# Decode-step kernel: queries' units before keys' units, decode ticks from the third key unit on

## The reference, cut to what matters

```python
h = rms_norm(x, kv_norm); proj = h @ kv_w
k = rms_norm(proj[keys], k_norm); v = proj[values]; logf = log_sigmoid(proj[forget] + f_bias)
qz = rms_norm(x, norm_g) @ w_q
q = rms_norm(qz[queries], q_norm); z = qz[gate]
s = q k^T / 8 + (c_q - c_k)          # c: cumulative sum of logf; masked: key position <= query's
o = softmax(s) @ v
out = (o * silu(z)) @ w_out
```

## Time and profile before

| | |
|---|---|
| median of three runs | 2490.41 us |
| profiled execution, its own time | 2492.78 us |
| its span | 2490.9 us |
| PE, DVE, ACT, POOL busy, share of the span | 89%, 53%, 38%, 43% |
| granted TensorE clock, mean | 0.958 |
| HBM read, written | 386.8 MB, 43.9 MB |

### The profile page before, as it was taken

How to read it: one execution, slowest core, us unless ns; L and a number is a source line. 1 busy time by engine, 2 the same in 40 slices (tenths; PEclk the granted TensorE clock), 3 DMA queues, 4 the chain that set the end, 5 groups by cost and what they waited for, 6 DMA issues and landing times.

```text
span 2490.9 us, 47081 instructions
## 1 busy us (share of the span) xinstructions
PE 2227.7 (89%) x16540; PEld 1915.5 (77%) x16540; DVE 1316.3 (53%) x1892; ACT 949.9 (38%) x1617; POOL 1076.7 (43%) x715
## 2 busy tenths in 40 slices
PE   5999999999339998979999999978888888898999
PEld 3999999999139998969999777745555455557998
DVE  4689888988690016566785111124443534444332
ACT  4556655665461013222222121424444344453121
POOL 0698899889673114443233333222222211211231
PEclk7999999999789999989999999989999998999999
DMA  3222222221143121133323778999999988972112
GB/s 112 65 69 78 78 65 68 80 76 63 37 126 119 44 102 43 66 119 111 117 76 121 267 266 332 331 369 397 348 378 391 358 334 328 399 288 106 50 60 83
DMA packets 137487, 430.96 MB, mean 173 GB/s; under 512 B 23889, under 2 KB 40658, under 8 KB 136162
## 3 DMA queue, kind: packets, MB, share of 16 engines
q1 hardware_dynamic: 121554, 375.94, 41.3%
q0 software_dynamic: 13168, 41.58, 4.7%
q10 hardware_dynamic: 2592, 11.14, 1.1%
HBM read 386.81 MB, written 43.87 MB: 173 GB/s over the span
## 4 chain that ended last, share of the span: by engine, by line
PE 58%; POOL 15%; DVE 11%; issue 8%; ACT 6%; DMA 2%; ACTq 0%; SPq 0%; POOLq 0%; DVEq 0%
POOL ACC L1346 7%; PE PS L602 6%; PE PS L600 6%; PE PS L601 6%; PE PS L698 5%; PE PS L700 5%; PE PS L699 5%; PE PS L821 4%; PE PS L765 4%; PE PS L874 3%; PE PS L901 3%; PE PS L889 2%; POOL ML L1376 2%; PE PS L608 2%; POOL WL L1319 2%
## 5 line engine op out<-in xcount | busy, mean ns | idle before, releaser
L1319 POOL TENSOR_TENSOR WL<-RAW,WH 128x1024 fp32r<-128x1024 f32 (+1 forms) x121 | 306.0, 2529 | 601.1 <-ACT WH L954 596.4
L1656 DVE SCALAR_TENSOR_TENSOR PS<-UX,CWT,PS 128x1024 f32<-128x1024 f32 (+1 forms) x672 | 466.2, 781 | 0.0
L633 PE MATMUL PS<-HH,WH 128*128 128x384 f32 (+1 forms) x1152 | 378.6, 329 | 20.7 <-DVE HL L1642 20.7
L635 PE MATMUL PS<-HH,WL 128*128 128x384 f32 (+1 forms) x1152 | 377.4, 328 | 0.0
L634 PE MATMUL PS<-HL,WH 128*128 128x384 f32 (+1 forms) x1152 | 377.3, 328 | 0.0
L1346 POOL TENSOR_TENSOR ACC<-ACC,PROD 128x1088 f32<-128x1088 f32 x112 | 284.7, 2542 | 31.3 <-ACT PROD L1006 25.1
L698 PE MATMUL PS<-GH,WH 128*128 128x384 f32 (+1 forms) x792 | 271.6, 343 | 26.4 <-DVE KC L1768 12.1
L700 PE MATMUL PS<-GH,WL 128*128 128x384 f32 (+1 forms) x792 | 263.1, 332 | 0.0
L699 PE MATMUL PS<-GL,WH 128*128 128x384 f32 (+1 forms) x792 | 262.1, 331 | 0.0
L633 PEld LDWEIGHTS PS<-HH,WH 128*128 128x128 f32 x1152 | 217.3, 189 | 24.7 <-issue 13.7
L954 ACT ACTIVATE WH<-RAW 128x1024 fp32r<-128x1024 f32 (+1 forms) x121 | 131.4, 1086 | 252.5 <-PE PS L602 217.0
(11 more groups left out here) (213 smaller groups left out, 4309.3 us busy)
## 6 DMA issues: line engine op xcount, KB each, us to landing
KV<-ck SPq DMA_DIRECT2D x256, 512.0 KB, 6.7
KV<-cv SPq DMA_DIRECT2D x256, 512.0 KB, 6.7
RAW<-wA SPq DMA_DIRECT2D x48, 512.0 KB, 3.3
RAW<-wP SPq DMA_DIRECT2D x16, 640.0 KB, 4.0
zT_scr<-ZS ACTq DMA_DIRECT2D x16, 544.0 KB, 2.7
Z<-zT_scr SPq DMA_DIRECT2D x16, 544.0 KB, 3.6
RAW<-wB SPq DMA_DIRECT2D x17, 512.0 KB, 3.2
RAW<-wO SPq DMA_DIRECT2D x16, 512.0 KB, 3.2
```

The lines of the kernel that those rows point to most:

```text
L633: pe.matmul(out, WH[w][:, kk], HH[:, k, a:b], start=k == 0, stop=False)
L635: mm = pe.matmul(out, WL[w][:, kk], HH[:, k, a:b], start=False, stop=k == KD - 1)
L1319: pool.tensor_tensor(WL[s][:, 0:n], RAW[s][:, 0:n], WH[s][:, 0:n].bitcast(F32), ALU.subtract).then_inc(s_lo, 1)
L1656: i = dve.scalar_tensor_tensor(out=o, in0=x, scalar=w[:, j:j + 1], in1=o, op0=ALU.mult, op1=ALU.add)
```

## The change

- The constants U_Q and U_K change places: the eight query units run before the eight key units. Weights' places, gains, scales and what is kept of the sample rows follow.
- 120 ticks instead of 72 lie in the units, listed by unit in UNIT_TICKS: 15 in the key units (2 to 3 in each from the third on), 41 in the value units, 64 in the gate units. 168 instead of 216 follow from the prompt stage's first slot on.
- The first batch has its new rows' scores at tick 15 instead of 1 (the new keys are complete only then), and its product with the new rows' values in a step of its own, `first_new`, at tick 68, with small tiles of its own (PTN0, OE0, OT0, RID0), since the values are complete only then. Its result is copied by `decode_heads(0)` at tick 71.
- The norm of queries and keys works in place in PSUM banks 0 to 2 (NCHAIN) instead of in SBUF (RS3); ACT takes one square root over 1088 columns instead of three; PE's next `norm` waits for DVE's product instead of ACT's root. FL now lies in the last part of SC.
- ACT's queue stores the normed rows, in `sample_columns`, not SP's. POOL loads the raw weights of the key units too. SP issues the first four page loads after the last query unit's weights.
- In ACT and DVE the ticks of a key unit stand before that unit's norm or scaling.
- On POOL the pads, the forget biases of batches 1 to 3 and `load_keys(0)` move, the last behind a wait for the first batch's end (`s_os`).

```diff
-U_CONV, U_OUT, U_PLE, U_F, U_K, U_Q, U_V, U_Z, U_W, U_TAIL = 0, 48, 64, 72, 73, 81, 89, 97, 105, 113
+U_CONV, U_OUT, U_PLE, U_F, U_Q, U_K, U_V, U_Z, U_W, U_TAIL = 0, 48, 64, 72, 73, 81, 89, 97, 105, 113
...
+        NCHAIN = PS[:, 0:3, :].rearrange("p a n -> p (a n)")[:, 0:R]
...
-        def unit_ticks(u):
-
-            if u < U_V + 2:
-                return 0, 0
-            return (4 * (u - U_V - 2), 4) if u < U_Z else (24 + 6 * (u - U_Z), 6)
-
-        SPOTS = {0: (), 4: (1, 3, 5, 7), 6: (1, 2, 3, 5, 6, 7)}
+        UNIT_TICKS = (0, 0, 2, 2, 2, 3, 3, 3) + (0, 1, 6, 6, 7, 7, 7, 7) + (8,) * PAIRS
+        SPOTS = {0: (), 1: (7,), 2: (3, 7), 3: (2, 5, 7), 4: (1, 3, 5, 7), 5: (1, 3, 4, 6, 7), 6: (1, 2, 3, 5, 6, 7),
+                 7: (1, 2, 3, 4, 5, 6, 7), 8: (0, 1, 2, 3, 4, 5, 6, 7)}
...
+        NEW_AT = (15,) + (1,) * (DB - 1)
+        I_FIRST = T_B + 32
+
+        T_UNITS, T_LEAD, T_END = sum(UNIT_TICKS), 4, T_B * DB + 4
+        H_UNITS = sum(i % T_B < 16 or 18 <= i % T_B < 34 for i in range(T_UNITS)) // 4 * 4
...
-            def store_normed(p):
-
-                sp.wait_ge(s_kn, p + 1)
-                sp.dma_start(kT[p] if p < PAIRS else qT[p - PAIRS], KN[:]).then_inc(s_kst, 16)
...
             def norm(p):
 
                 pe.wait_ge(s_sq3, p + 1)
-                atleast(pe, s_rs, p)
-                colsum(pe, 0, SQ3, w=BONES).then_inc(s_n, 1)
+                atleast(pe, s_kn, p)
+                for a, b in ((0, 512), (512, 1024), (1024, R)):
+                    mm = pe.matmul(NCHAIN[:, a:b], BONES, SQ3[:, a:b], start=True, stop=True)
+                mm.then_inc(s_n, 1)
...
+            def first_new():
+
+                pe.wait_ge(s_vr, PAIRS)
+                pe.wait_ge(s_dv, 18)
+                for y in range(4):
+                    mm = pe.matmul(PS[32 * y:32 * y + 32, 6, 0:4 * HD], PTN0[:, 32 * y:32 * y + 32],
+                                   VNW[:, 4 * HD * y:4 * HD * y + 4 * HD], start=True, stop=True)
+                mm.then_inc(s_fn, 1)
...
             def sample_columns(p):
 
                 act.wait_ge(s_kn, p + 1)
-                if p == PAIRS:
+                act.dma_start(qT[p] if p < PAIRS else kT[p - PAIRS], KN[:]).then_inc(s_kst, 16)
+                if p == 0:
                     act.wait_ge(s_pad2, 1)
...
             for p in range(2 * PAIRS):
-                weights_hi(U_K + p + 1)
+                weights_hi(U_Q + p + 1)
+                ticks(U_Q + p)
                 if p >= 2:
                     sample_columns(p - 2)
...
-                if U_V <= u + 3 < U_W:
+                if U_K <= u + 3 < U_W:
                     pool.wait_ge(s_lo, u + 2)
                     pool.dma_start(RAW[(u + 3) % 2][:, 0:KD * P], wB[wb(u + 3)]).then_inc(s_rawp[(u + 3) % 2], 16)
...
             pool.wait_ge(s_lo, U_W)
             pool.wait_ge(s_vst, 32 * PAIRS)
+            pool.wait_ge(s_os, 1)
             load_keys(0)
...
-                dve.reciprocal(RS3[:], RS3[:]).then_inc(s_rc, 1)
+                dve.reciprocal(NCHAIN, NCHAIN).then_inc(s_rc, 1)
...
             for p in range(2 * PAIRS):
+                ticks(U_Q + p)
                 atleast(dve, s_kn, p - 1)
-                scaled(KC[p % 2], U_K + p, 1, s_kc)
+                scaled(KC[p % 2], U_Q + p, 1, s_kc)
```

More of the change, by code:

```diff
@@ L531, in forget_back @@
                 sp.dma_start(FL[0:H, :], lfT).then_inc(s_fin, 16)
-            for u in range(U_F, U_V):
+            for u in range(U_F, U_K):
                 raw(u, wB[wb(u)], u % 2)
@@ L537, in _ @@
                     sp.dma_start(xS, X2[:]).then_inc(s_xs, 16)
-                if u == U_K + 4:
+                if u == U_Q + 4:
                     forget_store()
-                if u == U_K + 5:
+                if u == U_Q + 5:
                     forget_compact()
[L542 to L557, removed]
+            sp.wait_ge(s_xs, 16)
+            sp.wait_ge(s_gl, KD)
+            pages(0)
+            pages(1)
+            forget_logs()
+            forget_back()
+            pages(2)
+            pages(3)
             def raw_out(m):
@@ L1094, in unit @@
                     if not (end and l == 1):
-                        hi_next(u0, s, i, KD * P if end else SLOT, gained=end, less=PAIRS * l)
+                        hi_next(u0, s, i, KD * P if end else SLOT, gained=end, less=3 * PAIRS // 2 * l)
                     act.wait_ge(s_gate, KD * l + m + 1)
@@ L1222, in forget_exp, with ticks @@
                 act.activation(FC_E[:], FC_E[:], ACT.Exp).then_inc(s_fe, 1)
+            def ticks(u):
+                for k in range(KD):
+                    i = tick_after(u, k)
+                    if i is not None:
+                        decode_tick(i)
             for p in range(2 * PAIRS):
-                weights_hi(U_K + p + 1)
+                weights_hi(U_Q + p + 1)
+                ticks(U_Q + p)
                 if p >= 2:
@@ L1242, in _ @@
                     norm(2 * PAIRS - 1)
-                for k in range(KD):
-                    i = tick_after(u, k)
-                    if i is not None:
-                        decode_tick(i)
+                ticks(u)
             silu(PAIRS - 1)
@@ L1518, in _ @@
                     forget_out()
+                    scores_pad()
                 if p == PAIRS + 6:
```

142 lines of the change are left out of this document (88 added, 54 removed).

## The result

The kernel after takes 2527.9 us in the median (2526.6 to 2531.0, four runs) against 2489.9 for the kernel before beside it: a ratio of 1.0146 [1.0132, 1.0160]. It is slower by 38 us by the medians, 36 by the ratio, where +15 was forecast. The side is right, the size is off by more than a factor of two. The execution profiled after has a span of 2525.3 us against 2490.9, so the trace has 34.4 us to explain.

What follows compares the result with a forecast made beforehand. PE was taken to bound the units, with DMA time to spare, while the softmax chain idles PE in the prompt stage. Units +70 us and prompt stage -55 gave +15, forecast 2505 us; 8 in 10 between 2479 and 2528.

Steps and rivals of the forecast that it cites:

- what bounds each stretch: Units bound by PE with spare DMA time; in the prompt stage PE idles 81 us for the softmax chain, not pages.
- the sign: Whole kernel: slower, by 15 us or 0.6%; chance of slower 0.60, same 0.14, faster 0.26.
- Rival A: Prompt stage: ticks there cost more than their PE work, so the kernel gets faster, -13 us, 2477 us; chance 0.26.
- PE work of a tick: Units: 48 added ticks at 1.2 us of PE work each, +57.6 us.
- Pages: Units: page loads of dense gate units exceed the DMA rate, with a ring of four buffers; +9 us, bounds 0 and +30.
- rival B: Units: pages bind there, +30 us instead of +9, so +36, 2526 us; chance 0.20 together with C.
- Single bank set: Query, key and value units share banks and wait for DVE's scaling; with row maximum and forget scan, +3 us together.
- Rival C: Prompt stage: softmax chain rules all items, a removed tick gives 0.4 us; +37, 2527 us; chance 0.20 together with B.
- the -55 us of the prompt stage: Prompt stage: 48 ticks removed; ordinary ticks -41, batch changes -5, entry -9 us.
- Entry: Prompt stage's first item falls from 19.0 to about 10 us, its first ticks needing no page: -9 us (0 to -10).
- Items with ordinary ticks: Prompt stage: a removed tick gives 0.85 us over all, none in items of 896 and 1024 keys: -41 us.
- batch changes: Prompt stage: five batches instead of six pass their row maximum there: -5 us (0 to -6).

Runs made afterwards that it cites:

- experiment 6: Kernel before with six sample batches instead of eight and SP's wait at half group 184 of 192, so 144 prompt-stage ticks instead of 216: 2429.5 us, ratio 0.9748.
- experiment 1: Kernel after, with SP's wait for the last head pair's scores after half group 248 instead of 240 of 256: 2519.5 us, ratio 1.0105.
- experiment 3: Kernel after with the kernel before's tick counts (72 in the units, none in key units), all else kept: 2493.3 us, ratio 1.0011.
- experiments 5 and 10: Kernel before with 48 ticks in the units, none in value units: 2478.9 us; then 52, seven in each of the last four gate units: 2474.9 us.
- 84 ticks: Kernel after with 84 ticks in the units (20 value, 64 gate, no key) and SP's wait at half group 248: 2522.2 us, ratio 1.0128.
- the shifted kernel before: Kernel before with every prompt-stage tick due 0.7 of a slot earlier, nothing else: 2504.3 us, ratio 1.0049.
- experiment 2: Kernel after with one tick moved from the fifth gate unit to the last value unit, putting the third batch's row maximum inside a unit: 2528.1 us, ratio 1.0151.

## Why the prediction was right or wrong

**Right: what bounds each stretch, and the sign.** The units grew by 66.3 us, 1.38 for each of the 48 ticks: their full PE work and the stalls at unit ends. A tick taken from the prompt stage gives back less, because it filled the chain's gaps: 0.87 in experiment 6, and in experiment 1, with SP's wait gone, 614.3 - 571.8 = 42.5 us or 0.89, the entry in it. By the ratios the loss of 36 us splits into 3 for the order alone (experiment 3), 23 for the 48 ticks at their new places (3 to 1), and 10 for SP's wait (1 to the kernel after). The prices alone give 48 x (1.38 - 0.87) = 24.5 us. The two agree, but the placing of ticks moves single runs by 12 us and more, so this is not a proof to the microsecond. The opposite direction (experiments 5 and 10) confirms the sign, not the 0.87. Rival A, faster, has fallen.

**"PE work of a tick", right within 10%**: 57.6 forecast, +61.8 measured in PE's busy time. Key units with two ticks last 17.45 us where 17.8 was forecast.

**"Pages", over-sized**: 9 forecast, 2.1 us of PE's waits measured in the units. The DMA engines are at 0.99 there with 375 GB/s, and the ring of four buffers suffices; rival B has fallen. That 375 GB/s over 95 us and, in the stage of 52 ticks, 379 over 616 us were moved speaks again against the limit of 358 that the prediction quoted from the Trainium skill (DMA: Bandwidth & Descriptors, "Where 436 GB/s comes from"), at least for one core that runs alone.

**"Single bank set", +3 forecast and 2.4 measured, by luck.** Two more stalls were to cost 3.3 us and one row maximum 1.5. PE's waits for the scaling fell by 2.8 instead (12.1 to 9.3), and its waits for the first exponential rose by 5.2 (0.8 to 6.0), since the new one fell on a unit's first spot, behind ACT's work for the unit just ended. That was priced as an average one. With PE's work and the pages' 2.1 this makes up the 66.3 us.

**Rival C, the chain takes over**, lies between: the idle time in the stage did rise by 15 us, but without SP's wait the stage gave back twice the 0.4 a tick. Its 2527 us, and the end of the stated range at 2528, were met by the sum of other causes.

**The step that failed: the -55 us of the prompt stage.** The stage and the gap ahead of it gave back 34.3 us in the trace (37.0 less 2.7), so this sum is 21 us too large and carries nearly the whole error of 23. Two things are wrong in it.

*No term for SP's queue.* The prediction followed the page loads past the moved work in the units, and read SP's waits for buffers in the stage, but not the one row below them, the 8.3 us for the prompt's scores. That wait is tied to the prompt's progress, the page loads behind it to the ticks' progress; whoever changes the rate between the two (216 / 128 = 1.69 ticks a slot to 168 / 128 = 1.31) has to check it. It grew to 32.2 us and costs 8.4 us (experiment 1).

*What a tick gives back, priced too high.* Without SP's wait the stage and the gap still gave back only 39.8 us. "Entry": -9 forecast. The first item fell by 12.3 us, but the pages that it no longer waited for were waited for one and two items later. PE's waits from 1696 to 1741 us:

```profile
PE PS L824 <- DMA KV<-cv: 5.7, 3, 3.6
PE PS L761 <- DMA KV<-ck: 2.6, 2, 1.6
PE PS L803 <- ACT SC L1228: 1.4, 1, 1.4
PE PS L764 <- DMA KV<-ck: 1.1, 1, 1.1
```

The first four items together went from 48.6 to 42.9 us, and 2.7 more were lost between the last unit and the stage: 3 us won, not 9. "Items with ordinary ticks" and "batch changes": -41 and -5 forecast, 0.85 a tick and the changes on top. Experiment 6 gives 0.87 *with* its two batch changes, so that the two terms together should have been about -42; which of them was too large these runs do not tell.

**Open.** Why 84 ticks lie some 23 us above a straight line from 72 (experiment 3) to 120 (experiment 1), and why the shifted kernel before is slower. What experiment 2's edit is worth, and what the last 2 us in the end stage are, stay open too.

## What to carry to other kernels

Work that fills the gaps of a latency chain is cheap where it is, and full price in a stretch whose engine is never idle. Before moving it, price one piece at both places (here 1.38 against 0.87 us), by a run that drops pieces in one of them. When two progressions share an in-order queue, every wait in it that belongs to one of them is a bound on the other, and a change of their relative rate moves it; list such waits even if they cost nothing now. And where filler is dealt out by a formula, count what falls on which item, and deal it first to the items whose chain has gaps: a tick cost 0.29 to 0.54 us in a long item here and 1.08 to 1.27 in a short one. A shift of 0.7 of a slot was worth 24 us at one count, against 38 for the whole change.

## What was unexpected of the hardware

A single wait of 5.3 us, in a stretch where PE is otherwise always busy, was followed by 3.3 us of gapless matmuls at a clock of 0.50 and 4 us at 0.68. Before it and after it the clock is 1.00. The first item of the stage stands at 0.50 in the kernel after (0.55 before), behind 12.5 us in which PE was busy for two thirds:

```profile
1696.60:1709.10 12.50, 8.31 (x86) 2.90 (x86) 2.83 (x6) 3.05 (x5) 6.90 (x9) 0.77 0.82 320
```

The mean granted clock of those 12.5 us is 0.77.
